# Output projection of a hybrid decoder step: the residual rows are added by GpSimd instead of VectorE, and the turned mix lies 128 bytes further

## The reference, cut to what matters

```python
x = x + gt1 * (jnp.concatenate([att, conv], axis=-1) @ w_out)
h2 = rmsnorm(x, g_n2) * (1 + sc2) + sh2
# hierarchical_moe(h2): group logits and expert logits, top-1 of 4 groups,
# top-2 of 8 experts, then the experts
```

## Time and profile before

| what | value |
|---|---|
| time, median of 3 executions | 2188.47 us (2188.36 to 2189.56) |
| time of the profiled execution | 2188.47 us |
| span of the profiled execution | 2186.9 us |
| PE busy in the span | 1983.7 us (91%) |
| DVE busy in the span | 1582.0 us (72%) |
| ACT busy in the span | 1050.6 us (48%) |
| POOL busy in the span | 533.8 us (24%) |

### The profile page before, as it was taken

How to read it: one execution, slowest core, us unless ns; L and a number is a source line. 1 busy time by engine, 2 the same in 40 slices (tenths; PEclk the granted TensorE clock), 3 DMA queues, 4 the chain that set the end, 5 groups by cost and what they waited for, 6 DMA issues and landing times. The chain is left out here.

```text
span 2186.9 us, 40449 instructions
## 1 busy us (share of the span) xinstructions
PE 1983.7 (91%) x13272; PEld 1590.7 (73%) x13273; DVE 1582.0 (72%) x3149; ACT 1050.6 (48%) x2056; POOL 533.8 (24%) x571
## 2 busy tenths in 40 slices
PE   6999999998999987689999399999899998999976
PEld 3788888886787776378888278788687876778732
DVE  3558888986988888389998568664547674648757
ACT  2312111112888887144453267555436564647623
POOL 1013444430111153015654301001110101010055
PEclk8999999998999999789999599999999999999989
DMA  8686555665667577767777289975758797769978
GB/s 258 236 294 233 210 184 189 228 223 173 201 196 260 183 263 255 251 198 246 257 262 245 81 301 396 347 287 180 253 198 297 278 350 266 259 247 381 398 243 312
DMA packets 221315, 553.21 MB, mean 253 GB/s; under 512 B 28802, under 2 KB 43482, under 8 KB 219929
## 3 DMA queue, kind: packets, MB, share of 16 engines
q1 hardware_dynamic: 170891, 425.60, 55.6%
q0 software_dynamic: 25088, 75.71, 9.7%
q10 hardware_dynamic: 25239, 50.67, 6.7%
HBM read 456.95 MB, written 167.56 MB: 286 GB/s over the span
## 5 line engine op out<-in xcount | busy, mean ns | idle before, releaser
L2530 DVE TENSOR_TENSOR LO<-WIDE,HI 128x2048 fp32r<-128x2048 f32 x128 | 287.1, 2284 | 85.0 <-ACT HI L2452 85.0
L644 DVE SCALAR_TENSOR_TENSOR arena<-arena,tapw 128x512 f32<-128x512 f32 (+3 forms) x435 | 266.4, 691 | 0.0
L2452 ACT CAST HI<-WIDE 128x2048 fp32r<-128x2048 f32 x128 | 238.1, 1909 | 23.1 <-PEq L217 16.2
L2530 DVE TENSOR_TENSOR LO<-W2E,HI 128x2048 fp32r<-128x2048 f32 x64 | 143.8, 2289 | 93.3 <-ACT HI L2452 93.3
L445 POOL TENSOR_TENSOR STATS<-STATS,K 128x1 f32<-128x1 f32 x16 | 134.4, 8400 | 308.1 <-ACT H L497 308.1
L777 PE MATMUL PJ<-WIN_H,HTH 128*128 128x512 f32 x640 | 160.3, 392 | 5.0 <-ACT HTH L505 5.0
L787 PE MATMUL PJ<-WIN_L,HTH 128*128 128x512 f32 x640 | 158.7, 390 | 0.0
L781 PE MATMUL PJ<-WIN_H,HTL 128*128 128x512 f32 x640 | 158.2, 389 | 0.0
L2452 ACT CAST HI<-W2E 128x2048 fp32r<-128x2048 f32 x64 | 118.7, 1904 | 60.5 <-issue 60.5
L777 PEld LDWEIGHTS PJ<-WIN_H,HTH 128*128 128x128 f32 x640 | 118.6, 188 | 32.9 <-issue 9.1
L529 ACT ACTIVATE arena<-PJ 128x512 f32<-128x512 f32 x48 | 28.6, 601 | 231.5 <-PE PJ L787 231.5
(11 more groups left out here) (367 smaller groups left out, 4515.6 us busy)
## 6 DMA issues: line engine op xcount, KB each, us to landing
WIDE<-in_w_expert_gate SPq DMA_DIRECT2D x64, 1024.0 KB, 8.3
WIDE<-in_w_expert_up SPq DMA_DIRECT2D x64, 1024.0 KB
W2E<-in_w_expert_down SPq DMA_DIRECT2D x64, 1024.0 KB
expert_rows<-YE ACTq DMA_DIRECT2D x40, 512.0 KB
expert_rows<-NOROWS POOLq DMA_DIRECT2D x11, 1536.0 KB, 11.7
QN<-q_rows SPq DMA_DIRECT2D x48, 256.0 KB
KN<-out_new_k_prompt SPq DMA_DIRECT2D x48, 256.0 KB, 4.1
VN<-out_new_v_prompt SPq DMA_DIRECT2D x48, 256.0 KB, 3.9
```

The source lines that it names most:

```text
L644: ins = nc.vector.scalar_tensor_tensor(out=out, in0=src, scalar=tap, in1=out, op0=ALU.mult, op1=ALU.add)
L2452: nc.scalar.copy(HI[n][:, cols], raw[n][:, cols]).then_inc(hi_ready[n], 1)
L2530: nc.vector.tensor_tensor(LO[n][:, cols], raw[n][:, cols], HI[n][:, cols], ALU.subtract).then_inc(lo_ready[n], 1)
```

## The change

`added` disappears from VectorE. GpSimd gets `add_rows(i - 1)`, the same sum of the same rows, as the first thing in its round, ahead of `keep_weight` and `scale`. It waits for the same two semaphores (`x2_half` and the residual load) and raises the same one (`x2_ready`). Besides, a pad of 128 bytes for each partition is put between `MIX` and the turned mix `MT_H` / `MT_L`, so these and the tiles allocated behind them lie 128 bytes further.

```diff
-        MIX, MTH, MTL = sb("MIX", [P, D]), sb("MT_H", [P, KD, P], F32R), sb("MT_L", [P, KD, P], F32R)
+        MIX = sb("MIX", [P, D])
+        sb("MIX_PAD", [P, P // 4])
+        MTH, MTL = sb("MT_H", [P, KD, P], F32R), sb("MT_L", [P, KD, P], F32R)
...
+                def add_rows(i, rows):
+
+                    pool.wait_ge(x2_half, i + 1)
+                    pool.wait_ge(x_in, i * 16 + 16)
+                    pool.sem_inc(placing, 1)
+                    pool.tensor_tensor(X2[0:rows], X2[0:rows], X[0:rows], ALU.add).then_inc(x2_ready, 1)
+
                 def round_(i):
+                    if there(i - 1):
+                        add_rows(i - 1, rows_of(i - 1))
                     if there(i - 3):
                         keep_weight(i - 3)
...
-                def added(i, rows):
-                    dve.wait_ge(x2_half, i + 1)
-                    dve.wait_ge(x_in, i * 16 + 16)
-                    nc.vector.tensor_tensor(X2[0:rows], X2[0:rows], X[0:rows], ALU.add).then_inc(x2_ready, 1)
-
...
                         weigh(i - 3)
-                    if there(i - 1):
-                        added(i - 1, rows_of(i - 1))
                     if there(i):
                         att_rest(i)
```

More of the change, by code:

```diff
@@ L1633, in output_projection_and_routing @@
         LN, LNH, WR = sb("LN", [P, 2, KC]), sb("LNH", [P, 2, KC]), sb("WR", [P, KD, NR])
-        NB, ST, CC, X = sb("NB", [P, 3, DATT]), sb("STAT", [P, 3, 2 * HEADS]), sb("CC", [P, KC, P]), sb("X3", [P, D])
+        NB, ST, CC = sb("NB", [P, 3, DATT]), sb("STAT", [P, 3, 2 * HEADS]), sb("CC", [P, KC, P])
+        X = sb("X3", [P, D])
         BM, BE, BW, BT, BD, BRC = (sb("BM", [P, HEADS]), sb("BE", [P, 3, HEADS]), sb("BW", [P, 3, HEADS]), sb("BT", [P, 3, HEADS]), sb("BD", [P, HEADS]), sb("BRC", [P, HEADS]))
         BS, MV, VE, RS, YT, TH = sb("BS3", [P, 6]), sb("MV3", [P, 2]), sb("VE3", [P, 1]), sb("RS3", [P, 1]), sb("YT3", [P, KC, P]), sb("TH3", [P, KC, P])
-        MIX, MTH, MTL = sb("MIX", [P, D]), sb("MT_H", [P, KD, P], F32R), sb("MT_L", [P, KD, P], F32R)
+        MIX = sb("MIX", [P, D])
+        sb("MIX_PAD", [P, P // 4])
+        MTH, MTL = sb("MT_H", [P, KD, P], F32R), sb("MT_L", [P, KD, P], F32R)
         HA = KD // 2
```

## The result

The changed kernel takes 2207.36 us (median of 4, 2204.73 to 2209.01) against 2188.41 us for the kernel before: ratio 1.0086, 95% interval 1.0071 to 1.010, slower by 19 us. The forecast was 2195.6, the range ended at 2201. The direction was right and the size wrong by more than a factor of two. The profiled execution took 2207.09 us with a span of 2205.6.

The account below looks back on a forecast made before the run. DVE's gapless chain was taken to bound the projection's 15.95 us round, PE following by 0.17 to 0.19 us. Eleven rounds at 0.65 us gave +7.1 on 2188.47, so 2195.6 us; range for 8 in 10: 2190 to 2201.

Parts of the forecast that it names:

- DVE leads by 0.19 us, so little can be won: Output projection: DVE's chain sets the 15.95 us round; PE alone needs 15.76, so the stage wins at most 2.7 us.
- The sum takes 2.39 us and starts at the clearing transfer's end: Sum on POOL: starts at 1046.64 behind the clearing transfer's issue, takes 2.39 us, ends at 1049.03.
- Squares, scale, norm and loads are not late: Behind the sum: squares keep 0.26 us to spare; store and residual load move 1.5 us later, covered by the 15.95 us round.
- A narrow operation of DVE is held by POOL's wide one, inputs in PSUM are exempt, and so G's copy pays: DVE beside POOL's sum: MT_L and LOG run freely, the copy of 4 numbers is held until 1049.03.
- The step that failed: DVE's operations during POOL's sum, 1046.64 to 1049.03, were listed as MT_L, LOG and G's copy.
- The term of 0.65 us a round: DVE's MAX8 starts at 1049.12 instead of 1048.47, 0.65 us later; rounds go from 15.95 to 16.6 us.
- Eleven rounds, tiles 0 to 2 and 14 free: Hold costs only behind the 11 clearing transfers, tiles 3 to 13; tiles 0 to 2 lose nothing, tile 14's loss is covered.
- The rival "more is held": DVE beside the sum: LOG held too, +11.4 us, or a sum of 3.4 us, +18 us; chance 9% together.
- The pad at 0: Shifted tile addresses: no row depends on the pad; cost 0, within a few hundredths of a microsecond a round either way.

Follow-up runs that it names:

- e5: Changed kernel with weigh ahead of the gating, and G made by a second sum out of PSUM instead of copied from LOG: 2184.23 us, ratio 0.9986.
- e3: Changed kernel, but GpSimd copies the weights ahead of the sum: 2199.70 us, ratio 1.0049.
- e4: Changed kernel, but VectorE does the three tiny operations of weigh ahead of the gating: 2199.61 us, ratio 1.0050.
- e10: Changed kernel with a fill of 128x1024 on GpSimd between the clearing transfer and the sum, ahead of the sum's waits: 2217.79 us, ratio 1.0137.
- e11: Changed kernel with GpSimd's order behind the clearing transfer: fill of 128x1024, weights' copy, sum: 2211.57 us, ratio 1.0114.
- e8: Changed kernel, the clearing transfer moved behind the sum on GpSimd: 2202.13 us, ratio 1.0055.
- e7: Changed kernel, the sum on GpSimd split into two instructions of 512 columns, one behind the other: 2205.47 us, ratio 1.0077.

## Why the prediction was wrong

- *DVE leads by 0.19 us, so little can be won:* right for a round, not for the total. With nothing held but 0.14 us (e5) the round is 15.71, a little below the 15.76 given, which left out that the pad shortens TensorE's products by 0.27 us. TensorE still idles some 0.2 us before TPS there: TPS, logits, LOG (which waits 0.33 us for the logits) and DVE's chain form a ring, and it is that, not TensorE's work alone, that lasts 15.71. The total gain is 3.6 us where 2.7 was the bound: the bound counted eleven waits alone, and in the profiled execution of e5 the first and the last two steps of the stage give 2.7 us besides, the first by the clock, the last two in part by the pad.
- *The sum takes 2.39 us and starts at the clearing transfer's end:* right, 2.39 us.
- *Squares, scale, norm and loads are not late:* right; no wait for them appears.
- *A narrow operation of DVE is held by POOL's wide one, inputs in PSUM are exempt, and so G's copy pays:* right as a mechanism (e3, e4: 1.38 and 1.27 us; in the changed kernel itself it is seen at tile 1 alone, 0.59 us).
- *The step that failed:* "In the new order DVE does, while POOL adds from 1046.64 to 1049.03: MT_L (one input in PSUM), LOG (one input in PSUM), and then G<-LOG". The list of operations beside the sum was made from the sum's recorded start. W1R, with two inputs in SBUF, lies just ahead of it, and was taken as past. It was held, and with it MT_L and LOG lost their cover: MAX8 starts 0.98 us behind the sum's end (0.60 + 0.22 + 0.21, less the 0.05 by which MT_L starts ahead of that end) where the forecast had 0.09. The term of 0.65 us a round measured 1.48.
- *Eleven rounds, tiles 0 to 2 and 14 free:* tile 2 was not free. POOL was idle there when the gating ended, but W1R was held too, 2.38 us, since DVE reaches it 0.3 us after the gating, just as the sum starts; the step to tile 3 grew by 0.9. At tile 14 W1R was held as well (2.28 us), but the loss is covered by DVE's wait for TensorE, as forecast: the 1.4 us there go with the clock, which no term of the forecast had.
- *The rival "more is held":* its price of +11 to +18 us was near, its reason (LOG's input) was not: LOG ran at 0.18 to 0.20 us in every kernel. That the price was near is luck.
- *The pad at 0:* right in the time. That none of the rows depends on it was wrong (1.98 us for eight products instead of 2.03); it came out at 0 because VectorE leads.

## What to carry to other kernels

An operation moved from VectorE to GpSimd is not free because VectorE's list got shorter: as long as GpSimd reads SBUF for microseconds, each small VectorE operation with both inputs in SBUF, and each copy or scaling of a few columns within SBUF, is a stop. List what VectorE does from the moment at which the GpSimd operation's semaphores are met, not from its recorded start, and put only operations that read PSUM there. Putting a GpSimd operation that waits for the last of the tiny ones in front of the sum (e3), or moving the tiny ones ahead (e4), took the loss from 19 us to 11; moving them ahead and making the copy from PSUM (e5) turned it into a gain of 3.6. And before a step at the edge of a stage is put down to a change, compare the granted clock there.

## What the runs showed of the hardware that I had not expected

- A GpSimd operation that reads SBUF held a VectorE product from 0.37 us (changed kernel) and 1.27 us (e10) before its own recorded start, across a transfer's issue and a fill. DEN, also with two inputs in SBUF, started when the gating had just ended and ran 0.15 us in all of them. Where a copy that still waited for W1R stood in front of the sum, nothing was held early (e3, and e11 from tile 4 on). That the claim is made when the operation is handed over is my inference from this; the records show no such moment. How far ahead it reaches stays open: two operations ahead it is shown, but semaphores that are met may not be enough. At tile 3 of e8 the gating had ended at 998.21, W1R started at 998.50 during another transfer, with the experts' copy and the sum behind that, and took 0.16 us; the sum's recorded start is 999.49.
- Two GpSimd sums in a row without a wait kept the path as one where W1R started during the transfer in front of them (e7, 2.94 us for W1R), and let W1R through between them where it started beside the first of them (tiles 14 to 16, 1.19 to 1.20 us).
- A copy of 3 columns was held (1.28 us), operations of 1 column with a single input in SBUF were not (NG, 0.15 us).
- A pad of 128 bytes ahead of the turned mix took eight products of 128x512 from 2.03 to 1.98 us.
